# One program in place of three phases, in a hybrid recurrence and state-space block

## The reference, cut to what matters

```python
u = rms_norm(h, norm_g)
q, f_logit, iv, g_hg, u_s, z_s, gate_hg, gate_s5 = split(u @ w_in)        # 7168 columns
o = hgrn2_mix(q, f_logit, iv, lb)          # 8 heads, chunks of 64, state 128 x 128 carried in time
y_hg = (rms_norm(o, hg_norm_g) * silu(g_hg)) @ w_o_hg
ys = gelu(s5_mix(u_s, ...))                # 32 groups of 16 channels, 64 complex states each
a, b = split(ys @ w_glu + b_glu)
y_s5 = (a * sigmoid(b) * silu(z_s)) @ w_o_s5
h = h + (sigmoid(gate_hg) * y_hg + sigmoid(gate_s5) * y_s5) @ w_out
h = h + (p @ w_ple) * sigmoid(rms_norm(h, ple_norm_g) @ w_ple_gate)
return rms_norm(h, final_norm_g)
```

## Time and profile before

| | |
|---|---|
| median of 3 runs | 2324.18 us |
| range of the runs | 2321.78 to 2324.41 us |
| the profiled execution's own time | 2324.66 us |
| its span, first to last instruction | 2323.1 us |
| mean granted TensorE clock | 0.988 |
| TensorE matmul busy | 2241.4 us, 96% |
| VectorE busy | 1212.8 us, 52% |
| ScalarE busy | 916.5 us, 39% |
| GpSimd busy | 133.3 us, 6% |

### The profile page before, as it was taken

One profiled execution on the slowest core, in us unless ns is written; L12 is line 12 of the kernel. 1 busy time (PEld: TensorE's weight loads), 2 busy tenths in 40 slices (PEclk: granted clock), 3 DMA queues, 4 the chain that ended last, 5 costly groups with the idle time before them and its releaser, 6 DMA issues. The chain is left out here.

```text
span 2323.1 us, 30152 instructions
## 1 busy us (share of the span) xinstructions
PE 2241.4 (96%) x10758; PEld 1824.4 (79%) x10758; DVE 1212.8 (52%) x2251; ACT 916.5 (39%) x1359; POOL 133.3 (6%) x238
## 2 busy tenths in 40 slices
PE   7999999999999999979999999979999999999997
PEld 5788888888888888868777777757888777778875
DVE  5534344434343444432665656546567566665755
ACT  5434344434343444421333333333344353354343
POOL 0000000000000000000111111110002001100100
PEclk9999999999999999999999999989999999999998
DMA  6211010101010100022222222274337535633722
GB/s 209 53 48 43 18 46 9 45 9 45 14 45 18 36 24 31 10 74 73 81 90 86 81 75 85 76 231 158 116 111 233 160 96 181 201 112 121 238 91 82
DMA packets 104628, 206.38 MB, mean 89 GB/s; under 512 B 37216, under 2 KB 46432, under 8 KB 104544
## 3 DMA queue, kind: packets, MB, share of 16 engines
q1 hardware_dynamic: 85072, 143.87, 19.6%
q0 software_dynamic: 19472, 61.37, 7.8%
HBM read 157.87 MB, written 46.14 MB: 88 GB/s over the span
## 5 line engine op out<-in xcount | busy, mean ns | idle before, releaser
L95 PE MATMUL s_ps<-u_hi,s_w_hi 128*128 128x512 f32 x640 | 255.6, 399 | 8.9 <-DVE s_w_lo L950 8.9
L96 PE MATMUL s_ps<-u_lo,s_w_hi 128*128 128x512 f32 x640 | 250.2, 391 | 0.0
L97 PE MATMUL s_ps<-u_hi,s_w_lo 128*128 128x512 f32 x640 | 249.7, 390 | 0.0
L1528 DVE TENSOR_TENSOR t_w_lo<-c_raw,t_w_hi 128x1024 fp32r<-128x1024 f32 x136 | 166.5, 1225 | 83.7 <-ACT t_w_hi L1434 83.6
L95 PE MATMUL t_ps<-t_oa_hi,t_w_hi 128*128 128x512 f32 x512 | 201.5, 394 | 7.9 <-DVE t_oa_lo L1559 3.8
L97 PE MATMUL t_ps<-t_oa_hi,t_w_lo 128*128 128x512 f32 x512 | 200.4, 391 | 0.0
L96 PE MATMUL t_ps<-t_oa_lo,t_w_hi 128*128 128x512 f32 x512 | 200.4, 391 | 0.0
L1434 ACT ACTIVATE t_w_hi<-c_raw 128x1024 fp32r<-128x1024 f32 x136 | 142.6, 1049 | 70.8 <-DMA c_raw<-w_o_hg_in 28.7
L95 PEld LDWEIGHTS s_ps<-u_hi,s_w_hi 128*128 128x128 f32 x640 | 120.4, 188 | 47.9 <-issue 14.5
L97 PEld LDWEIGHTS s_ps<-u_hi,s_w_lo 128*128 128x128 f32 x640 | 120.4, 188 | 26.0
L96 PEld LDWEIGHTS s_ps<-u_lo,s_w_hi 128*128 128x128 f32 x640 | 120.6, 188 | 23.4
(11 more groups left out here) (290 smaller groups left out, 4741.1 us busy)
## 6 DMA issues: line engine op xcount, KB each, us to landing
c_raw<-w_in_in SPq DMA_DIRECT2D x54, 512.0 KB, 3.8
gates_scratch<-s_stage POOLq DMA_DIRECT2D x64, 256.0 KB, 2.7
t_ein<-gates_scratch SPq DMA_DIRECT2D x64, 256.0 KB, 4.2
c_raw<-w_o_hg_in SPq DMA_DIRECT2D x32, 512.0 KB, 4.3
c_raw<-w_out_in SPq DMA_DIRECT2D x32, 512.0 KB, 3.5
c_raw<-w_ple_gate_in SPq DMA_DIRECT2D x32, 512.0 KB, 3.5
c_raw<-w_glu_in SPq DMA_DIRECT2D x16, 512.0 KB, 3.8
t_xa<-o_gated_scratch POOLq DMA_DIRECT2D x32, 256.0 KB, 4.5
```

Source lines behind the costliest of these rows:

```text
L95: pe.matmul(out, w_hi, u_hi, start=first, stop=False)
L96: pe.matmul(out, w_hi, u_lo, start=False, stop=False)
L97: return pe.matmul(out, w_lo, u_hi, start=False, stop=last)
L1528: dve.tensor_tensor(w_lo[:, half], raw[:, half], w_hi[:, half].bitcast(F32), ALU.subtract).then_inc(w_lo_done, 1)
```

## The change

There is one block, one queue for each engine and one meeting point at the very end. The phases become parts (`Part`), whose queues are written one behind the other; what used to be implied by the meeting points is now waited for by name. The eight PSUM banks, the raw buffer and the two rounded weight buffers (`Weights`) are shared by all parts, and their counters run on (`W0`, `L0`).

- The last recurrence step is cut into quarters, one behind each tile of gate block 0. Blocks 0 and 1 have their weights rounded and split during the last head's last step.
- Pairs 0 to 15 run beside blocks 2 to 17. Blocks 2 and 3 are still `z` blocks. Blocks 18 and 19 stand without a pair. The parameters are computed during block 1; their loads, the first input load and GpSimd's constants wait for the recurrence's last store.
- The closing part's first inputs are loaded once all `ys` are stored, and rounded and split behind tile 1 of block 19; its first weights are split in block 19 and the second behind its end. Its first gate loads wait for block 19's stage stores, whose place in SBUF they take. The load of `h` waits for the last projection.

```diff
@@ part_head
+        wb_hi = m.sb("wb_hi", [P, 2, KT, P], F32R)
+        wb_lo = m.sb("wb_lo", [P, 2, KT, P], F32R)
+        w_hi = lambda kind: (w.hi, wb_hi)[kind // 2][:, kind % 2]
...
             heads(sp, head)
-            sp.wait_ge(w_lo_done, HEADS * 4 + 2)
-            prefetch(sp, c, [a["w_in"][ZB], a["w_in"][ZB + 1]])
+            for i in range(2):
+                sp.wait_ge(w_lo_done, HEADS * 4 + i + 1)
+                sp.dma_start(raw[:, i], a["w_in"][ZB + i]).then_inc(raw_in[i], 16)
             sp.wait_ge(y_done, STEPS)
             sp.dma_start(a["o_gated"][HEADS - 1, :, (NT - 1) * TT:], y[:]).then_inc(last_out, 16)
             sp.wait_ge(last_out, 16)
...
-            turn(STEPS - 1, False)
-            outer(STEPS - 1)
-            attend(STEPS - 1, False)
-            mean_square(STEPS - 1)
+            def last_step(quarter):
+                if quarter == 0:
+                    turn(STEPS - 1, False)
+                elif quarter == 1:
+                    outer(STEPS - 1)
+                elif quarter == 2:
+                    attend(STEPS - 1, False)
+                else:
+                    mean_square(STEPS - 1)
+            return last_step
...
+                if quarter == 0:
+                    turned_iv(STEPS - 1)
+                elif quarter == 1:
+                    scale_states(STEPS - 1, False)
+                elif quarter == 2:
+                    square_out(STEPS - 1, False)
+                else:
+                    act.preload_act_table_set("natural_log_exp_and_others")
+                    root_out(STEPS - 1)
@@ part_s5
         def slots(engine, body):
-            for b in range(Z_BLOCKS):
-                body(b, None, b % 2, b == 0, False)
-            for p in range(2):
-                body(Z_BLOCKS + p, p, p, p == 0, False)
-            with engine.Fori(1, PAIRS // 2 - 1) as i:
+            for b in range(Z_BLOCKS + 2):
+                body(b, b - AHEAD if b >= AHEAD else None, b % 2, b < Z_BLOCKS)
+            with engine.Fori(1, (PAIRS - Z_BLOCKS) // 2) as i:
                 for r in range(2):
-                    body(i * 2 + (Z_BLOCKS + r), i * 2 + r, r, False, False)
-            for p in (PAIRS - 2, PAIRS - 1):
-                body(Z_BLOCKS + p, p, p % 2, False, p == PAIRS - 1)
+                    body(i * 2 + (Z_BLOCKS + r), i * 2 + (Z_BLOCKS - AHEAD + r), r, False)
+            for b in range(PAIRS, NB):
+                body(b, b - AHEAD if b < PAIRS + AHEAD else None, b % 2, False)
...
@@ part_s5, SyncE
+            def body(b, p, r, z):
+                load_weights(b + 2, r)
+                if is_at(b, 0):
+                    for sem, value in head_over:
+                        sp.wait_ge(sem, value)
+                    for dst, src in ((are[:], a["s5_a_re"]), (aim[:], a["s5_a_im"]), (bre[:], a["s5_b_re"]), (bim[:], a["s5_b_im"]),
+                                     (cre[:], a["s5_c_re"]), (cim[:], a["s5_c_im"]), (dd[:], a["s5_d"]),
+                                     (dt[0:NS], a["s5_log_dt"][0:1].to_broadcast([NS, PAIRS])),
+                                     (dt[NS:P], a["s5_log_dt"][1:2].to_broadcast([NS, PAIRS]))):
+                        sp.dma_start(dst, src).then_inc(par_in, 16)
+                    load_u(0, 0)
...
@@ part_s5, TensorE
+                if p is None:
+                    for t in range(NT):
+                        project(b, r, t)
+                        if is_at(b, 0):
+                            last_step(t)
+                    return
...
@@ part_s5, ScalarE
+                    act.activation(stage[:, t], ps[t][:], ACT.Sigmoid).then_inc(sig_done if z else staged, 1)
+                    if t == 0 and not is_at(b, 0):
+                        round_weights(b + 1, 1 - r)
+                    if is_at(b, 0):
+                        last_step(t)
+                    if is_at(b, 1) and t == 1:
+                        parameters()
+                    if is_at(b, NB - 1) and t == 1:
+                        tail_inputs()
...
@@ part_s5, VectorE
+                if p is not None:
+                    matrices, angles, taps, states = pair(p, r, is_at(p, 0))
+                    matrices()
+                    angles()
+                if z:
+                    gated(b, 0)
+                if is_at(b, 0):
+                    last_step(0)
+                else:
+                    split_weights(b + 1, 1 - r)
+                if is_at(b, NB - 1):
+                    tail_inputs()
+                if p is not None:
+                    taps()
+                if z:
+                    gated(b, 1)
+                    if b == 0:
+                        last_step(1)
+                    elif b == 1:
+                        parameters()
+                if p is not None:
+                    states()
+                if z:
+                    for t in (2, 3):
+                        gated(b, t)
+                        if b == 0:
+                            last_step(t)
@@ part_tail
-        ps = [m.ps(f"ps{i}") for i in range(BANKS)]
-        ms = [m.ps(f"ms{i}") for i in range(2)]
+        ps, ms = banks[4:8] + banks[0:2], banks[2:4]
...
+                    if sec == "glu" and not body:
+                        sp.wait_ge(*s5["stored"][quarter])
...
+            for sem, value in s5["y_out"]:
+                sp.wait_ge(sem, value)
             for k in range(S5KT):
                 sp.dma_start(xa[:, k], y_source(k, 0)).then_inc(first_xa_in[k], 16)
-            prefetched(sp, c, 1, raw_in)
...
                 if n == len(XPRO) - 3:
+                    pool.wait_ge(*s5["projected"])
                     load_h(0)
@@ build
-            phase_head(nc, c, a, xs, u_hi, u_lo)
-            phase_s5(nc, c, a, u_hi, u_lo)
-        phase_tail(nc, c, a)
+            head = part_head(nc, c, a, w, banks, xs, u_hi, u_lo)
+            s5 = part_s5(nc, c, a, w, banks, u_hi, u_lo, head.handed_on["drained"], head.handed_on["over"])
+        tail = part_tail(nc, c, a, w, banks, s5.handed_on)
+        block = m.block()
...
+        @block.scalar
+        def _(act):
+            last_step = head.scalar(act)
+            first_inputs, rest = tail.scalar(act)
+            s5.scalar(act, last_step, first_inputs)
+            rest()
```

More of the change, by code:

```diff
@@ L97, in split_matmuls, with __init__, part_head @@
     return pe.matmul(out, w_lo, u_hi, start=False, stop=last)
[L100 to L116, removed]
+class Part:
+    def __init__(self, sync, gpsimd, tensor, scalar, vector, **handed_on):
+        self.sync, self.gpsimd, self.tensor, self.scalar, self.vector = sync, gpsimd, tensor, scalar, vector
+        self.handed_on = handed_on
+def part_head(nc, c, a, w, banks, xs, u_hi, u_lo):
     FIRST = 4
@@ L402, in head @@
                     recur = not (first and t == 0)
-                    split = t == NT - 1 and not last
+                    split = t == NT - 1
                     act.wait_ge(proj_done, n * 4 + 1)
@@ L429, in head @@
                     act.activation(iv[:], pi[:], ACT.Copy).then_inc(iv_done, 1)
-                    if split:
+                    if split and not last:
                         round_weights(h + 1, 2)
                     if recur:
-                        norm(n - 1, first and t == 1)
-                    if split:
+                        square_out(n - 1, first and t == 1)
+                        root_out(n - 1)
+                    if split and not last:
                         act.wait_ge(proj_done, n * 4 + 4)
@@ L834, in _, with tensor, project @@
             slots(pool, body)
-            for r in range(2):
-                pool.wait_ge(ys_out[r], 16 * PAIRS - 32 * r)
-        @block.tensor
-        def _(pe):
-            def project(b, r, t, first, ks=range(KT)):
-                if not first and ks[0] == 0:
+        def tensor(pe, last_step):
+            def project(b, r, t, ks=range(KT)):
+                if is_at(b, 0):
+                    pe.wait_ge(*drained[t])
+                elif ks[0] == 0:
                     pe.wait_ge(staged, (b - 1) * NT + t + 1)
@@ L862, in body @@
                     for q in range(2):
                         rows = slice(q * NS, (q + 1) * NS)
-                        for k in range(2):
-                            ins = pe.matmul(py[q][0:GC, NCK:NCK + P], bb[rows, k],
-                                            Z[rows, k, 0:SC].rearrange("p j c -> p (j c)"), start=k == 0, stop=k == 1)
-                    ins.then_inc(mats_done, 1)
-                project(b, r, 1, head, range(3, KT))
-                project(b, r, 2, head, range(0, 2))
```

411 lines of the change are left out of this document (209 added, 202 removed).

## The result

The changed kernel takes 2294.5 us, the median of 4 runs (2289.95 to 2296.14); the kernel before, run beside it, 2324.3 us. The ratio is 0.987, with a 95% interval of 0.985 to 0.989. A second set of runs, with the experiments, gave 2293.98 us and a ratio of 0.9876 (0.9857 to 0.9895). The forecast was 2294.5 us in a range of 2290 to 2302. The profiled execution took 2296.14 us.

A forecast was written before the change was run, and what follows sets the result against it. TensorE was the bound, busy 2241.4 of 2323.1 us. From 2324.66 us, less 15.35 and 15.06 for the joins, plus 0.8 for a new wait, came 2295.05; the median's 0.48 us offset gave 2294.5 us, range 2290 to 2302.

The forecast's parts named there:

- First join: Recurrence's last step into gate block 0: interleaving it with the block's tiles and dropping the restart saves 15.35 us.
- Second join: Last pair's output product to the closing part's first matmuls: covering that chain with gate blocks saves 15.06 us.
- Rival 3: Something, such as a shared buffer, still holds a phase boundary's first matmul: 12 or 15 us come back; chance 0.05.
- Added wait: Block 2, pair 0: its late start makes TensorE wait 0.8 us for the states, bounds 0 and 4 us.
- a wait on the matrices: Block 2: TensorE waiting on the matrices was listed as a sign that the prediction was wrong; no size given.
- rival 2: Pair 0 later than drawn, as SyncE's issues and ScalarE's waits line up: 4 to 6 us; chance 0.10.
- The stretch kept as it is: Closing part's second four units, 1547.42 to 1576.00 us: the 6.82 us lost there stay, 4 less to 5 more.
- Rival 1: Closing part's start: transfers take back part of the gain, 4 us more, 2298.5 us; chance 0.12.
- Rival 4: Pair blocks: each pair's chain overruns its block, so all 16 wait; 3 us each gives 2342 us; chance 0.03.
- TensorE's busy time was to fall by 4 us: Whole profile, a sign of being right: TensorE's busy time smaller by 4 us, for slow matmuls count as busy.
- One clock dip at the start of the program alone: Whole profile, a sign of being right: TensorE's clock dips once, at the program's start, and nowhere else.
- the trace does not bear out a slow clock behind short pauses: Block 2's new wait: no clock restart expected, citing 1547 to 1576 us; otherwise 1.6 to 2.6 us on top.

## Why the prediction was right, step by step

- **First join, 15.35 us.** 15.37 measured. The recurrence step costs 5.28 us in line: block 1 begins 27.04 us after block 0, and four tiles are 21.76. The cover, VectorE and ScalarE behind each tile, holds: 28.00 of 28.00 us busy.
- **Second join, 15.06 us.** 14.20 us net of pair 0's wait in block 2, so 14.9 us. It was not held by the first gate load, nor by a stage store. Rival 3 did not happen.
- **Added wait, 0.8 us.** The transposes stand 7.84 us into block 2 (7.48 before) and the output product 24.75 (24.06 before): 0.7 us. The size is right, the place only in part. The prediction had the matrices just in time and all of the wait at the states or the copies; half of the delay already stands at the transposes, whose wait for the matrices (0.20 us) is the only one that the list names. By the prediction's own list a wait on the matrices was a sign of being wrong; at this size it changes nothing. The links of the drawing came up to 0.7 us later than drawn (y ready to store at 4.5 us into block 1, weights rounded from 10.7, first exponential 14.4, parameters done 23.2), and the start of the matrices at 24.45 us was drawn at 23.9. The later kernel with the chain one tile late shows that it has no slack to speak of: rival 2 is real as a mechanism, and 4 us away.
- **The stretch kept as it is, 6.82 us.** 6.48 us. The pattern moved along as assumed, with its 13.19 us weight load; with the residual load moved out of the stretch 4.7 us of it are gone. Rival 1, more contention from the later loads, did not happen.
- **Rival 4, all pairs late.** The list has one wait of a pair, in block 2.
- **The sum.** 2294.5 us against 2294.5 and 2293.98. That the sum meets the measurement to 0.1 us is luck: single terms were off by up to 0.3 us, the closing part took 1.6 us more in one profile and 0.2 in the other, and the runs of the changed kernel spread over 6 us. What is not luck is that each of the two joins came within 0.2 us of its term.

Besides the wait on the matrices, three signs were forecast wrongly, and all three are about the clock. TensorE's busy time was to fall by 4 us, for both cold restarts. Between the first join and the last os5 unit it did (560.7 to 556.4 us), but in all it fell by 1.8, since the closing part has slow stretches of its own, of another size in each run (716.1 us busy before, 718.8 and 716.8 after). "One clock dip at the start of the program alone" is wrong: 1920 to 1940 us has 0.83, behind the loop's pause, and the kernel before had slow matmuls at the same place, behind the wait of 3.52 us. And the sentence that the trace does not bear out a slow clock behind short pauses was right only for the stretch that it cited. The same trace of the kernel before shows matmuls of 0.63 us behind waits of 3.52, 2.55 and 3.07 us, at 1962, 2010 and 2265 us; in the later runs 3.71 us in block 2 and 2.85 us at the loop were enough. It did no harm, because the new wait was only 0.2 us.

## What to carry to other kernels

A phase boundary costs less for its meeting point (3.2 and about 2.4 us here, with the rounding and splitting of the weights behind it) than for the chain that nothing covers: the last step's waits, the store, the reload, and the slow clock behind them. So overlap the chains; whether there is a barrier matters last. A step that already runs between matmuls elsewhere can be priced exactly by its pitch there. Behind the joins look at big transfers on another queue and at the jump of a hardware loop: here small waits of 1 to 3 us cost as much in slow matmuls as in idle time, or more.

## What the runs showed of the hardware

- The cold restart is not of one size: 1.55 us behind the first join before and 2.56 us behind the 12.5 us of the second, 2.97 us when TensorE rested 5.33 us in one piece behind a step with small waits, 1.6 us behind 11.5 us, 1.7 us behind 3.71 us.
- Nor does the length of a short pause decide whether there is one. At the loop's jump, pauses of 1.85 us (residual load of tile 0 in pieces), 2.37 us (second profile) and 2.85 us (first profile) were followed by 8, 8 and 14 matmuls of some 0.63 us; one of 2.51 us at the same place, with all residual loads in pieces, by none.
- 512 KB of weights landed in 13.2 us beside one 2 MB load of another queue in time tile 0, and in 8.3 and 10.7 us in tile 1. In tile 1 it was 4.1 to 5.0 us with the same bytes in eight pieces on the queue of the weights.
